# Low weight parts of a hybrid decoder trunk by GpSimd, the S5 input product by VectorE, half of a branch projection behind the S5 matrices

## The reference, cut to what matters

```
for l in (0, 1):
    u_a, u_b, z_ga, z_gb = split(x @ w_in + b_in)              # 512, 512, 1024, 1024 wide
    out_a = (window means of u_a, minus u_a) @ w_pool * pool_scale
    h     = complex linear recurrence: lam_bar * h + b_bar @ u_b # S5, 32 groups of 64 states
    y     = gelu(real(c @ h) + d_skip * u_b);  out_b = y * sigmoid(y @ w_glu + b_glu)
    m     = (sigmoid(z_ga) * (out_a @ w_proj_a) + sigmoid(z_gb) * (out_b @ w_proj_b)) @ w_out
    x     = layer_norm(ALPHA * x + m)
    f     = (silu(x @ wg) * (x @ wu)) @ wd                     # l = 0: dense, 2816 wide
    f     = sum of the top 2 of 8 experts' SwiGLU              # l = 1: 3584 wide
    x     = layer_norm(ALPHA * x + f)
```

## Time and profile before

| | us |
|---|---|
| median of 3 runs (1801.79 to 1802.01) | 1801.89 |
| the profiled execution | 1799.7 |
| its span, first to last instruction | 1798.0 |
| PE busy | 1659.2 (92%) |
| DVE busy | 1374.6 (76%) |
| ACT busy | 1001.9 (56%) |
| POOL busy | 105.5 (6%) |

### The profile page before, as it was taken

The page is one execution under the profiler, slowest core; times in us unless marked ns, Lnnn a source line. Parts: engine busy times, 40 slices in busy tenths (PEclk is TensorE's granted clock), DMA queues, the critical chain, the costliest instruction groups (busy, mean ns, idle before and its releaser), DMA issues.

```text
span 1798.0 us, 25620 instructions
## 1 busy us (share of the span) xinstructions
PE 1659.2 (92%) x9595; PEld 1413.1 (79%) x9595; DVE 1374.6 (76%) x1459; ACT 1001.9 (56%) x910; POOL 105.5 (6%) x101
## 2 busy tenths in 40 slices
PE   6677989899996969899999999999999999999994
PEld 4676689898986938788888888888888888888883
DVE  7883266758577235699898898998898988988986
ACT  3331235343343203577777777777777777777771
POOL 2412000000014010200000000000000000000000
PEclk9888699999998958999999999999999999999997
DMA  6243073454533313499999999899899999998990
GB/s 178 74 135 87 15 207 119 142 190 139 187 101 110 109 26 121 166 327 365 336 346 379 324 358 370 317 365 377 316 368 355 327 378 327 356 378 308 368 354 24
DMA packets 209696, 441.84 MB, mean 246 GB/s; under 512 B 22896, under 2 KB 26912, under 8 KB 209614
## 3 DMA queue, kind: packets, MB, share of 16 engines
q1 hardware_dynamic: 205230, 434.40, 68.5%
q0 software_dynamic: 2432, 5.34, 1.5%
q10 hardware_dynamic: 1968, 1.19, 0.3%
HBM read 437.06 MB, written 1.93 MB: 244 GB/s over the span
## 4 chain that ended last, share of the span: by engine, by line
PE 75%; DVE 16%; issue 4%; DMA 2%; ACT 1%; POOL 1%; DVEq 0%; ACTq 0%
PE bank L1576 71%; PE bank L1579 3%; DVE piece_lo L959 3%; DVE ssm L959 2%; DVE r_all L959 2%; DVE w_lo L959 2%; DVE scr L959 1%; POOL ssm L645 1%; DVE wide L1193 1%; ACT y_hi L896 1%; DMA piece<-in_w_out_dram 0%; DMA ssm<-ssm 0%; DVE turn L959 0%; DVE wide L959 0%; DVE tiny L959 0%
## 5 line engine op out<-in xcount | busy, mean ns | idle before, releaser
L959 DVE TENSOR_TENSOR w_lo<-weights,w_hi 128x2048 fp32r<-128x2048 f32 x336 | 765.1, 2289 | 99.0 <-ACT w_hi L905 94.6
L905 ACT ACTIVATE w_hi<-weights 128x2048 fp32r<-128x2048 f32 x336 | 644.4, 1920 | 190.9 <-PE bank L1576 190.8
L1576 PE MATMUL bank<-w_hi,xg_hi 128*128 128x512 f32 x896 | 357.4, 399 | 3.9 <-DVE xg_lo L959 2.5
L1576 PE MATMUL bank<-w_hi,xg_lo 128*128 128x512 f32 x896 | 350.7, 391 | 0.0
L1576 PE MATMUL bank<-w_lo,xg_hi 128*128 128x512 f32 x896 | 350.0, 391 | 0.0
L1576 PE MATMUL bank<-x_hi,piece_hi 128*128 128x264 f32 x672 | 199.7, 297 | 45.1 <-DVE piece_lo L959 38.7
L717 ACT ACTIVATE piece_hi<-piece 128x1024 fp32r<-128x1024 f32 x130 | 134.3, 1055 | 180.2 <-PE bank L1576 148.8
L959 DVE TENSOR_TENSOR piece_lo<-piece,piece_hi 128x1024 fp32r<-128x1024 f32 x130 | 162.3, 1274 | 90.8 <-ACT piece_hi L717 87.2
L1576 PEld LDWEIGHTS bank<-w_hi,xg_hi 128*128 128x128 f32 x896 | 168.6, 188 | 43.4 <-DVE w_lo L959 4.8
L1576 PE MATMUL bank<-x_hi,piece_lo 128*128 128x264 f32 x672 | 197.8, 294 | 0.0
L1576 PEld LDWEIGHTS bank<-w_hi,xg_lo 128*128 128x128 f32 x896 | 168.5, 188 | 36.8
(11 more groups left out here) (293 smaller groups left out, 1997.8 us busy)
## 6 DMA issues: line engine op xcount, KB each, us to landing
weights<-in_w_moe_gate_dram SPq DMA_DIRECT2D x112, 1024.0 KB, 7.3
weights<-in_w_moe_up_dram SPq DMA_DIRECT2D x112, 1024.0 KB, 7.3
weights<-in_w_moe_down_dram SPq DMA_DIRECT2D x112, 1024.0 KB, 6.5
piece<-in_w_in_dram SPq DMA_DIRECT2D x48, 512.0 KB, 4.1
piece<-in_w_ffn_gate_dram SPq DMA_DIRECT2D x22, 512.0 KB, 4.5
piece<-in_w_ffn_up_dram SPq DMA_DIRECT2D x22, 512.0 KB, 4.4
piece<-in_w_ffn_down_dram SPq DMA_DIRECT2D x22, 512.0 KB, 3.6
piece<-in_w_out_dram SPq DMA_DIRECT2D x16, 512.0 KB, 4.4
```

The lines of the kernel that those rows point to most:

```text
L905: act.activation(w_hi[s % PAIRS][:, :], ring_slot[:, :], ACT.Copy).then_inc(w_hi_ready, 1)
L959: return dve.tensor_tensor(out, a, b, op)
L1576: signals(pe.matmul(out, lhsT, rhs, start=start, stop=stop, skip_group_check=True), signal)
```

## The change: what it does

1. `low_by` gives each split piece an owner for its low part: DVE keeps the first two pieces and the 22 of `down`, POOL gets the other 106. POOL has its own semaphore; SP and PE wait for the owner's. POOL's list per layer: `ub`, `ua`, `gate`, then the output DMAs and the Toeplitz DMAs, then `out`, then in layer 0 the 44 dense pieces. In layer 1 its pieces stand behind the wait for the last `down` tile and the fill of `utok`.
2. The S5 input product moves from POOL to DVE, behind `pooling` (and behind `s5_outputs` in layer 0).
3. PE and DVE do the second half of `pa` behind `s5_matrices` and `kernel_rows`.
4. ACT makes the high parts of one piece behind the variance, and of the rest up to the limit ahead of channel block 3, in each layer norm; before, it did so behind the layer norm.
5. The `next_lo` calls in `s5_tables`, `pooling` and in layer 0's `s5_outputs` are gone.

```diff
+    low_by = ["d" if j < 2 or plan[i][0][0] == "down" else "p" for j, i in enumerate(split_plan)]
...
+        def wait_split(eng, j):
+            eng.wait_ge(w_lo_ready if low_by[j] == "d" else w_lo_of_pool, low_place[j] + 1)
...
@@ POOL
-            def s5_inputs(l):
...
+            def weights_lo(*which):
+                for j, i in enumerate(split_plan):
+                    key, _, k, n, _ = plan[i]
+                    if low_by[j] == "p" and key[:len(which)] == which:
+                        pool.wait_ge(w_hi_ready, j + 1)
+                        pool.tensor_tensor(piece_lo[j % RAWS][:, 0:k * n], piece[i % RAWS][:, 0:k * n],
+                                           piece_hi[j % RAWS][:, 0:k * n], ALU.subtract).then_inc(w_lo_of_pool, 1)
...
-                s5_inputs(l)
+                    pool.wait_ge(utok_zero, 2)
+                weights_lo("ub", l)
+                weights_lo("ua", l)
+                weights_lo("gate", l)
...
+                weights_lo("out", l)
+                if l == 0:
+                    for c in range(len(FGROUPS)):
+                        weights_lo("w_ffn_gate", c)
+                        weights_lo("w_ffn_up", c)
@@ ACT, layer_norm
+                weights_hi(min(n_hi + 1, split_limit["var", l, which]))
...
                 for k in range(KD):
+                    if k == 3:
+                        weights_hi(split_limit["var", l, which])
@@ DVE
+            def s5_inputs(l):
+                wait_emptied(dve, ("ut", l, 2))
+                product(w1n, False, powv, bbar, CHUNK, prod[0]).then_inc(w1n_ready, 1)
+                dve.wait_ge(w1n_ready, l + 1)
...
                 pooling(l)
                 if l == 0:
-                    s5_outputs(0, ("mix", 0, 0))
+                    s5_outputs(0)
+                s5_inputs(l)
...
+                first_branch(range(4))
                 kernel_rows(l)
+                first_branch(range(4, KD))
@@ PE
-                for c in range(2):
-                    project(("pa", l, c), rows_of(oaT), lambda k: wait_emptied(pe, ("mix", l, k)))
+                project(("pa", l, 0), rows_of(oaT), lambda k: wait_emptied(pe, ("mix", l, k)))
                 s5_matrices(l)
+                project(("pa", l, 1), rows_of(oaT))
```

More of the change, by code:

```diff
@@ L172, in psum_plan @@
         tiles += [(("h0", l, r), "a") for r in range(2)] + [(("rows", l, s), "a") for s in range(2)]
-        tiles += [(("mix", l, g), "a") for g in range(4)] + [(("pa", l, m), "d") for m in range(KD)]
-        tiles += s5_matrices(l) + [(("chunk", l, r), "d") for r in range(3)]
+        tiles += [(("mix", l, g), "a") for g in range(4)] + [(("pa", l, m), "d") for m in range(4)]
+        tiles += s5_matrices(l) + [(("pa", l, m), "d") for m in range(4, KD)] + [(("chunk", l, r), "d") for r in range(3)]
         tiles += [(("y", l, i), "ad"[i % 2]) for i in range(4)]
@@ L1079, in angles, with s5_tables @@
                 step(tt(FI, FI, T0, ALU.mult))
-            def s5_tables(l, before):
+            def s5_tables(l):
                 L = slice(NQ * l, NQ * l + NQ)
@@ L1129, in c_rows, with product, between @@
                 dve.memset(bpair, 0.0).then_inc(bpair_zero, 1)
-            def s5_outputs(l, before):
-                wait_emptied(dve, ("ct", l, 1))
[L1133 to L1140, removed]
-                next_lo(before)
-                tt(vmat[1], pw[0], mt[1], ALU.mult)
-                next_lo(before)
-                step(tt(t4, pw[1], mt[0], ALU.mult))
-                next_lo(before)
-                flat = [x.rearrange("p q n c -> p (q n c)") for x in (vmat[1], t4)]
-                dve.scalar_tensor_tensor(out=flat[0], in0=flat[0], scalar=-1.0, in1=flat[1],
-                                         op0=ALU.mult, op1=ALU.subtract).then_inc(vmat_ready, 1)
-                next_lo(before)
+            def product(out, minus, powers, mat, n, scratch, before=None):
+                def between():
+                    if before:
+                        next_lo(before)
+                pw = [powers[:, r, :, :].unsqueeze(3).to_broadcast([P, NQ, n, GC]) for r in range(2)]
+                mt = [mat[:, r, :, :].unsqueeze(2).to_broadcast([P, NQ, n, GC]) for r in range(2)]
+                t4 = scratch[:, 0:NQ * n * GC].rearrange("p (q n c) -> p q n c", q=NQ, n=n)
+                tt(out[0], pw[0], mt[0], ALU.mult)
+                between()
+                step(tt(t4, pw[1], mt[1], ALU.mult))
+                between()
+                step(tt(out[0], out[0], t4, ALU.subtract))
+                between()
+                tt(out[1], pw[0], mt[1], ALU.mult)
+                between()
+                step(tt(t4, pw[1], mt[0], ALU.mult))
+                between()
+                if not minus:
+                    return tt(out[1], out[1], t4, ALU.add)
+                flat = [x.rearrange("p q n c -> p (q n c)") for x in (out[1], t4)]
+                return dve.scalar_tensor_tensor(out=flat[0], in0=flat[0], scalar=-1.0, in1=flat[1],
+                                                op0=ALU.mult, op1=ALU.subtract)
@@ L1150, in s5_outputs @@
+            def s5_outputs(l, before=None):
+                wait_emptied(dve, ("ct", l, 1))
+                product(vmat, True, powr, ctr, NPOW, prod[l], before).then_inc(vmat_ready, 1)
                 dve.wait_ge(vmat_ready, l + 1)
@@ L1323, in mixer, with first_branch @@
                 if l == 0:
[L1324 to L1330 removed]
+                    s5_outputs(0)
+                s5_inputs(l)
+                def first_branch(ms):
+                    for m in ms:
+                        wait_emptied(dve, ("gate", l, m))
+                        dve.scalar_tensor_tensor(out=mT[:, m, :], in0=gates[:, m, :], scalar=1.0,
+                                                 in1=trunk_tile(("pa", l, m))[:, 0:T], op0=ALU.add, op1=ALU.mult)\
+                            .then_inc(emptied["d"], 1)
+                first_branch(range(4))
                 kernel_rows(l)
+                first_branch(range(4, KD))
                 states(l)
```

44 lines of the change are left out of this document (16 added, 28 removed).

## The result

| | before | after |
|---|---|---|
| median, us | 1801.84 (1801.23 to 1802.01) | 1826.42 (1817.7 to 1827.5, 4 runs) |
| ratio | | 1.0126, 95% interval 1.0095 to 1.0158 |
| the profiled execution, us | 1799.7 | 1827.16 |
| its span, us | 1798.0 | 1825.1 |

The change makes the kernel 1.3% slower. The forecast of 1798.5 was wrong, and 1826.42 lies outside its range of 1781 to 1813.

A forecast was written before the change was run, and what follows sets the result against it. The trunk was taken as bound by PE where fed, and by DVE's list order at gate-stage starts. Terms -3.5 - 1.0 + 2.3 + 2.8 + 11.2 - 15.2 = -3.4 us gave 1798.5 us; range 1781 to 1813.

The forecast's parts named there:

- Layer 0 up to `y`: -3.5: Start to layer 0's `y`: `w1n` ready at 140.4, PE not in the way, `y` at 178.6 against 182.06, -3.5 us.
- rival (1): Layer 1's gates: POOL takes turns with DVE's product and falls behind PE, -15.2 becomes about -5, total 1808; chance 0.25.
- The half projection by itself: 0: Second half of `pa` behind the S5 matrices: only reorders PE's time, brings forward Toeplitz DMAs nobody waits for, 0 us.
- Both `out` stages: -0.5 each: `out` in both layers: low part no longer behind DVE's residual additions, though POOL takes 1.1 us longer; -0.5 us each.
- Layer norms: +2.3 and +2.8: Layer 0's norm and layer 1's input norm: POOL's subtractions hold up DVE's scalings, high parts cost ACT time; +2.3, +2.8 us.
- Dense part: +11.2: Dense part: layer 1's tables on DVE wait for POOL, PE stands 14 us and starts cold; `down` 0; +11.2 us in all.
- Layer 1 up to `y`: -15.2: Layer 1's gates to `y`: PE fed by POOL, -18.1 us less 2.9 for turns with the product, -15.2.
- The price of a low part: A 1024-wide low part on POOL: 2.33 us, bounds 1.9 to 2.6, replacing 1.15 us net of DVE time.
- the lock itself: A DVE operation reading two SBUF tiles waits for POOL's running operation to end, gets one turn, then waits again.
- the warning drawn from the Trainium skill: VectorE and GpSimd share an exclusively locked SBUF port pair; this speaks against 106 more POOL operations beside DVE's.
- Rival (2): POOL's low parts, all stages: quicker than taken, 1.9 us each, total 1783; chance 0.18.
- Rival (4): Start of `y`: Toeplitz DMAs bound it, so the half projection gives 7.2 us a layer, total 1784; chance 0.04.

The follow-up runs named there:

- e7: The kernel after, but layer 0's `ub`, `ua` and `gate` low parts made by DVE at their old places and between both products' operations: 1806.77 us, ratio 1.0015.
- e5: The kernel before with only the second half of the branch projection moved behind the S5 matrices in both layers: 1813.2 us, ratio 1.0046.
- e2: The kernel after with both halves of the branch projection ahead of the S5 matrices again: 1813.82 us, ratio 1.0052.
- e11: The kernel before plus the S5 product on DVE with low parts between, high parts made ahead in the norms, `out` low parts on POOL: 1780.93 us, 0.9867.
- e4: The kernel before with only the S5 input product moved to DVE, low parts between its steps, all low parts by DVE: 1775.68 us, ratio 0.985.
- e8: The kernel after without high parts made inside the layer norms, only behind a whole norm as before: 1830.53 us, ratio 1.0148.
- e3: The kernel after, but the 44 dense gate and up low parts by DVE, two places for them in layer 1's tables: 1813.56 us, ratio 1.0055.
- e10: The kernel after, but layer 1's `ub`, `ua` and `gate` low parts by DVE, in pooling and between the product's operations: 1815.84 us, ratio 1.0065.
- e12: The kernel before, half projection moved behind the S5 matrices, `pb` loads and Toeplitz DMAs held back until the last `chunk` tile: 1811.61 us beside 1803.24 of before.
- e6: The kernel before, PE's order unchanged, `pb` loads held back until the second `kern` tile is filled: 1808.32 us, ratio 1.002.
- e9: The kernel before, half projection moved behind the S5 matrices, `pb` loads held back until the last `chunk` tile is filled: 1807.3 us, ratio 1.0016.
- e1: The kernel after, but POOL makes its 106 low parts by zero fills of about the same length, reading no SBUF: 1753.14 us, ratio 0.9726.

## Why the prediction was wrong

It was 30.5 us off on the span (-3.4 forecast, +27.1 measured). By its own steps:

- **Layer 0 up to `y`: -3.5** is the step that failed most; measured +11.3. Its sum for DVE was right: `w1n` ready at 140.4 forecast, 139.75 measured, with the price of 2.33 and 22 pieces. The sentence that failed is "PE is not in the way: the columns end at 72 instead of 56, its gates run from 74 to about 123". They began at 77.7 and ended at 142. I had charged each meeting of the two engines to DVE alone, whose operations wait for POOL's. But DVE had the six operations of `s5_outputs` and the six of the product in that time, 2.3 to 2.55 us each, and each also holds POOL up: 3.87 us a low part, where PE wants one in 2.94. Of the 15 us by which the gates overran their 49, PE stood 10.0 for POOL, and the rest is the lower clock behind these waits and behind the one for the columns. This is rival (1), which the prediction looked for only in layer 1's gates and gave 0.25; it named its deciding point rightly (a period of 2.9) and did not hold layer 0's list against it, though the twelve long operations stood in its own sum. e7 shows it: with those low parts on DVE, 16.8 us come back ahead of the transposes. Price of the step: 152.1 against 142.9 (140.4 and a cold start of 2.5), 9.2 us, and the stall below, 5.4.
- **The half projection by itself: 0** failed too; +5.4 and +4.8 us in after, +8 by e5, -13 by e2. The prediction asked who waits for the Toeplitz DMAs that it brings forward, and rightly found nobody. It did not ask what runs beside them. The two `pb` loads, whose buffers now come free only with the late half, and the Toeplitz DMAs then fill the DMA engines from before the start of `chunk`, and an instruction packet comes late. Before, the Toeplitz DMAs ran in `chunk` too, but only from its fourth microsecond, when that packet had landed.
- **Both `out` stages: -0.5 each.** Measured +2.8 and -0.2 from `y` to the mean, which holds more than `out` and scatters by as much. e11 points to a loss (+0.9 and +2.1 against e4), the second of them about at the edge of the scatter, so no run shows the gain that was forecast: POOL needs 2.33 us where DVE needs 1.22.
- **Layer norms: +2.3 and +2.8.** Measured +3.5 and +3.9, by the mechanism named: behind the variance a DVE scaling of 0.43 us takes 2.63, beside POOL's low part. The price of edit 4 is only part of it (e8: 2.2 in layer 1, not to be told in layer 0), and what it gives back further on, 5.1 and 3.2 us, was not in the sum as such.
- **Dense part: +11.2.** Measured +12.7, and that they are so close is partly luck. The mechanism was right for the gate and up groups: the stall of PE was forecast at 14 and a cold start and came as 12.8, and e3 gives 7.1 us back. But these groups lost 8.5 us, not 11.2, and "The `down` stage and `s5_outputs` of layer 1 have no POOL work beside them: 0" failed: `down` lost 4.1, most likely by the low part that `product` no longer makes.
- **Layer 1 up to `y`: -15.2.** Measured -7.5, of which +4.8 is the stall in `chunk`. Without it -12.2, 3 us short of the forecast. The sum had set aside 2.9 for the turns with the product, and e10, which takes them away, gets 4.3 us back.
- The sum of what was missed: 14.8 in layer 0, 4.8 and 3.0 in layer 1, 3.6 in the `out` stretches, 2.3 in the norms, 1.5 in the dense part (4.1 more in `down`, 2.7 less in front of it): 30.0 of 30.5.

**The price of a low part** and the lock itself were right, and so was the warning drawn from the Trainium skill. Rival (2), a quicker POOL, is refuted by 2.39 us alone. Rival (4), the Toeplitz DMAs as the bound of `y`, is refuted by the 13.2 us that stand before `y` in every kernel but e12.

## Why data DMAs stop PE inside chunk

The DMA table of short windows (queue, kind: packets, MB, share of 16 engines) shows it best in layer 1. In each kernel one packet of the instruction queue has to travel early in `chunk`. Before, it lands in the window 627.2 to 629.2 us, 2 to 4 us after the start of `chunk`, and has the engines almost to itself. In after there is none in the first 6 us, and it lands in 653 to 655, 6 to 8 us after the start, in a crowd; PE stands from 653.6 to 656.7. First the window of before, then that of after:

```profile
q0 software_dynamic: 13, 0.05, 27.0%
q8 instruction: 1, 0.02, 3.0%
```
```profile
q1 hardware_dynamic: 169, 0.34, 78.6%
q0 software_dynamic: 39, 0.06, 16.1%
q8 instruction: 1, 0.02, 4.2%
```

The same two windows in the other kernels: 2 to 4 us in e2 and e12 (no gap), 4 to 6 in e6 (gap 1.13), 6 to 8 in e5 (3.93). In e9 it is at 2 to 4 but takes twice the time (5.5% of 16 engines for 2 us instead of 2.7 to 3.0%), gap 0.92. So a late or slow packet and the gap go together in seven kernels. The gap stands behind the same matmul in all of them, within one, as the end of a block of code would.

The packed traces hold the start and end of every packet, and they tie the two closer. In all 18 gaps (nine kernels, two layers) the matmuls go on 1.3 to 1.9 us after the end of the packet: in after it ends 7.6 us behind the start of layer 0's `chunk`, and PE goes on at 9.0. In the five kernels without a gap (before, e2, e4, e11, e12) it ends 2.6 to 3.4 us behind the start, at least 2 us before PE reaches that matmul. e9 and e12 differ only in when the Toeplitz DMAs run, and in layer 0 the packet starts 4.1 us behind the start of `chunk` in e9 and 1.7 in e12.

The Trainium skill (Runtime: NRT & Kernel Launch, "Instruction fetch mechanics") says that instructions are fetched in blocks of 16 KiB by a DMA queue of their own, and that the cost of crossing from one to the next is "mostly hidden". The packet of 0.02 MB agrees. The cost does not: 0.8 to 4.8 us of standing here. It is hidden where the packet finds free DMA engines, as in before, whose Toeplitz DMAs start 3.7 us into `chunk`; with half of the projection in front of `chunk` they start 3.6 us ahead of it.

What stays open: the trace does not say which engine's code a packet carries, so that it is PE's is inferred from how its end and PE's next matmul go together. Why the granted clock falls when it does, 5.2 to 8.5 us behind the start of `chunk` in every kernel, no run here shows.

## What to carry to other kernels

Where two engines take turns on a lock, compute the period of both: the one moved work to pays the other's operation, as long as the list lasts. Ask it at each stage in which the consumer has a pace of its own (here PE, one piece in 2.94 us), and hold every rival against every stage, not only the one where it came to mind. Where the other engine's operation takes part in the lock, moving it there did not pay in this kernel: interleaved on one engine (2.29 + 1.22 us) the two were done sooner than on two engines in turns. When a function is rewritten in passing, as `s5_outputs` was, compare what it did with what it does: here some 3.4 us of `down` in each of nine kernels probably hang on it. And a moved matmul moves the release of its buffers, and so loads: look at what they then travel beside.

## What was not expected of the hardware

- GpSimd fills of the same length cost DVE's operations of two SBUF inputs nothing; subtractions that read SBUF cost the kernel 72 us more over 106 uses (e1).
- Copies with a single SBUF operand take part as well, even against fills: 64x512 in 2.47 us beside POOL's subtraction, 0.42 without it (e4), a 128x16 copy in 2.27, and 128x32 copies in 0.60 on average beside fills (e1), 0.19 without.
- The granted clock fell to 0.50 in a run of short matmuls without any gap (e12: from 5.7 us behind the start of `chunk`), and again behind short gaps (e6: 82 matmuls in 4.54 us behind 0.84).
- Loads that nobody waits for stopped PE for 0.8 to 4.8 us, by all signs through the instruction packet that they delayed.
